# Filled slots only through an indirect gather and scatter, and the experts' down product in high and low parts, in a two-layer block with 32 experts

## The reference, cut to what matters

```python
expert_id = (grp_idx * EXPERTS_PER_GROUP + top_i).reshape(-1)      # 1024 assignments in all
weights = grp_p * top_p / jnp.sum(top_p, axis=-1, keepdims=True)
...
def expert_block(args):
    xe, e = args                                                   # the tokens of expert e
    hid = jax.nn.silu(xe @ w_gate[e]) * (xe @ w_up[e])
    return hid @ w_down[e]
...
y = jnp.einsum('tkd,tk->td', y_assign.reshape(n_tok, TOP_K, d), weights.astype(yb.dtype))
```

## Time and profile before

| | |
|---|---|
| median of 3 runs | 3261.04 us (3250.35 to 3279.0) |
| the profiled execution | 3276.96 us, its span 3275.2 us |
| PE busy | 2789.9 us (85%) |
| PE weight load busy | 1775.8 us (54%) |
| DVE busy | 1397.0 us (43%) |
| ACT busy | 1001.0 us (31%) |
| POOL busy | 177.4 us (5%) |
| HBM traffic over the span | 129 GB/s mean |

### The profile page before, as it was taken

How to read it: one execution, slowest core, us unless ns; L and a number is a source line. 1 busy time by engine, 2 the same in 40 slices (tenths; PEclk the granted TensorE clock), 3 DMA queues, 4 the chain that set the end, 5 groups by cost and what they waited for, 6 DMA issues and landing times. The chain is left out here.

```text
span 3275.2 us, 30824 instructions
## 1 busy us (share of the span) xinstructions
PE 2789.9 (85%) x10792; PEld 1775.8 (54%) x10792; DVE 1397.0 (43%) x2100; ACT 1001.0 (31%) x1619; POOL 177.4 (5%) x200
## 2 busy tenths in 40 slices
PE   7899977479999779799996999848988999698885
PEld 1455455247777547457774444424755767444442
DVE  1104177532223235532355555532563234555554
ACT  1101221132222243532222444413353222244441
POOL 0000000000000010000000212100100000021110
PEclk9899988789999889989997999978999999799997
DMA  8401110013212212012223999941111222299994
GB/s 303 137 26 52 52 49 1 30 52 103 81 47 90 81 52 78 26 67 75 78 73 112 346 319 335 317 158 52 55 49 52 90 77 67 93 328 328 323 323 143
DMA packets 262816, 419.14 MB, mean 128 GB/s; under 512 B 17503, under 2 KB 179311, under 8 KB 262639
## 3 DMA queue, kind: packets, MB, share of 16 engines
q1 hardware_dynamic: 236448, 340.55, 31.6%
q10 hardware_dynamic: 17807, 47.76, 3.9%
q0 software_dynamic: 8448, 29.37, 3.0%
HBM read 390.37 MB, written 31.20 MB: 129 GB/s over the span
## 5 line engine op out<-in xcount | busy, mean ns | idle before, releaser
L180 PE MATMUL banks<-arena_parts,hT_parts 128*128 128x512 f32 x1056 | 442.6, 419 | 37.8 <-DVE ring_parts L210 26.3
L2537 DVE TENSOR_TENSOR ring_parts<-ring,hT_parts 128x2048 fp32r<-128x2048 f32 x128 | 292.5, 2286 | 302.4 <-ACT hT_parts L2453 302.2
L182 PE MATMUL banks<-arena_parts,ring_parts 128*128 128x512 f32 x1056 | 419.5, 397 | 0.0
L156 PE MATMUL banks<-ring,arena 128*80 128x512 f32 (+3 forms) x776 | 361.0, 611 | 15.5 <-DMA ring<-in_w_mod 11.4
L180 PE MATMUL banks<-hT_parts,arena_parts 128*80 128x512 f32 (+1 forms) x816 | 336.2, 412 | 43.9 <-DVE hT_parts L2534 18.6
L210 DVE TENSOR_TENSOR ring_parts<-ring,hT_parts 128x1024 fp32r<-128x1024 f32 x148 | 181.3, 1225 | 422.2 <-ACT hT_parts L206 419.5
L181 PE MATMUL banks<-ring_parts,arena_parts 128*80 128x512 f32 (+1 forms) x880 | 355.5, 404 | 0.0
L2453 ACT ACTIVATE hT_parts<-ring 128x2048 fp32r<-128x2048 f32 x128 | 243.9, 1907 | 355.2 <-DMA ring<-in_w_exp_up 330.9
L181 PE MATMUL banks<-hT_parts 128*128 128x512 f32 x864 | 345.2, 400 | 0.0
L206 ACT ACTIVATE hT_parts<-ring 128x1024 fp32r<-128x1024 f32 x148 | 156.6, 1058 | 479.3 <-PE banks L182 478.5
L180 PEld LDWEIGHTS banks<-arena_parts,hT_parts 128*128 128x128 f32 x1056 | 200.8, 190 | 113.4 <-issue 65.5
(11 more groups left out here) (435 smaller groups left out, 3198.0 us busy)
## 6 DMA issues: line engine op xcount, KB each, us to landing
ring<-in_w_exp_gate SPq DMA_DIRECT2D x64, 1024.0 KB, 6.8
ring<-in_w_exp_up SPq DMA_DIRECT2D x64, 1024.0 KB, 10.5
ring<-in_w_exp_down SPq DMA_DIRECT2D x128, 512.0 KB, 8.5
ring<-in_w_in SPq DMA_DIRECT2D x58, 1024.0 KB, 7.1
ring<-in_w_mod SPq DMA_DIRECT2D x24, 1024.0 KB, 7.9
y_rows<-arena ACTq DMA_DIRECT2D x64, 320.0 KB, 6.1
ring<-in_w_gate SPq DMA_DIRECT2D x11, 1024.0 KB, 5.5
ring<-in_w_up SPq DMA_DIRECT2D x11, 1024.0 KB, 8.0
```

The source lines that it names most:

```text
L156: last = nc.tensor.matmul(out, l, r, start=(i == 0), stop=(i == len(pairs) - 1))
L180: nc.tensor.matmul(out, lh, rh, start=start and i == 0, stop=False)
L182: last = nc.tensor.matmul(out, ll, rh, start=False, stop=stop and i == len(terms) - 1)
L2537: return V.tensor_tensor(half_of(ring_r, n, h), half_of(ring, n, h), ew_hi[:, h, :, :].bitcast(F32), ALU.subtract)
```

## The change

**Slots.** The tables now hold the token of an assignment plus one (assignments 0 to 1023), so that an empty slot gives -1. `tok_tab` holds the token, `row_tab` the assignment, and both gather and scatter pass a bounds check that leaves an index of -1 out. The first slot of a block is always filled, with token 0 and a spare row 1024 where no token is there. The ranks of a block are spread over its partitions (`slot_rank`). Results go by an indirect scatter on POOL to `y_rows` in the order of the assignments, so the combine reads `y_rows` with eight plain DMAs on ACT. `xg` is zeroed once in each layer. The fill of spare rows of `y_rows` before the scan (`fill_act`, four DMAs, 1792 KB) is gone, and two small DMAs of POOL at the start open the semaphores `yb_out0/1`. In the routing eight small DVE operations in five dependent groups follow the table's product where one cast did, and two that made `row_i` are gone.

**Down product.** It goes through `mm3`: twelve fp32r matmuls in place of four fp32 ones. ACT makes the high part of the down weights (`down_hi`), DVE the low part in place (`down_lo`) and the low part of the turned hidden rows (`hidden_lo`).

**Row copy.** `copy_rows` moves from DVE to ACT, and waits there for the scatter of two experts before (`yb_out`).

```diff
-            def rows_out(c, w):
+            def rows_out(c, n):
+                w = dn_rows(ring_r, n)
                 for h in range(2):
-                    last = mm(ps[0:CAP, 4 + h, :], [(e_ht[:, c, f, :], w[:, f, h * HB:(h + 1) * HB]) for f in range(2)])
+                    at = slice(h * HB, (h + 1) * HB)
+                    last = mm3(ps[0:CAP, 4 + h, :], [(ht_hi[:, c, f, :], ht_lo[:, c, f, :], dn_hi[:, f, at], w[:, f, at]) for f in range(2)], True, True)
...
-            def down(b, c, n, it):
-                j, r = ex_down(n), R + it
-                landed(pe, j, r)
+            def down(b, c, n):
+                pe.wait_ge(S("ex_dl"), b + 1)
                 pe.wait_ge(S("ex_ht"), b + 1)
                 pe.wait_ge(S("ex_yb"), b + 1)
...
             def body(b, c, n, it):                      # ACT
+                d_hi(b - 1, n - 1, it)
                 w_hi(b + 1, n + 1, it, 0)
                 silu(b, c)
                 x_hi(b + 1, 1 - c)
                 w_hi(b + 1, n + 1, it, 1)
+                rows(b - 1, 1 - c)
                 copy_h(b, c)
-                store(b - 1, 1 - c)
...
             def last():                                 # ACT
                 b = NE - 1
+                d_hi(b - 1, b - 1, 0)
                 silu(b, 1)
+                rows(b - 1, 0)
+                d_hi(b, b, 0)
                 copy_h(b, 1)
-                store(b - 1, 0)
-                store(b, 1)
+                rows(b, 1)
...
             def body(b, c, n, it):                      # DVE
+                d_lo(b - 1, n - 1)
                 w_lo(b + 1, n + 1, 0)
                 mult(b, c)
                 x_lo(b + 1, 1 - c)
                 w_lo(b + 1, n + 1, 1)
-                rows(b - 1, 1 - c, n - 1, it)
+                h_lo(b, c)
...
+            def rows(b, c):                             # ACT
+                act.wait_ge(S("ex_dn"), b + 1)
+                act.wait_ge(S(f"yb_out{c}"), yb_done(b, c, lay))
+                copy_rows(c).then_inc(S("ex_yb"), 1)
...
+            def put(b, c):                              # POOL
+                g.tensor_copy(row_cur[c], column(row_tab, b))
+                pool.drain()
+                return g.indirect_dma_start(out=y_rows, out_offset=bass.IndirectOffsetOnAxis(ap=row_cur[c].bitcast(U32), axis=0),
+                                            in_=yb[:, c, :], in_offset=None, bounds_check=2 * LAT, oob_is_err=False)
...
-            with pool.Fori(0, NE // 2 - 1, 1) as it:
+            gather(2, 0)
+            gather(3, 1)
+            with pool.Fori(0, NE // 2 - 2, 1) as it:
                 for c in range(2):
-                    gather(it * 2 + (c + 2), c)
+                    gather(it * 2 + (c + 4), c)
+                    scatter(it * 2 + c, c)
+            for b in range(NE - 4, NE):
+                scatter(b, b % 2)
...
-                    g.indirect_dma_start(out=comb[:, i, j, :], out_offset=None, in_=y_rows,
-                                         in_offset=bass.IndirectOffsetOnAxis(ap=row_i[:, j * LT + i:j * LT + i + 1].bitcast(U32), axis=0)).then_inc(S(f"comb_in{i}"), 16)
+                    act.dma_start(comb[:, i, j, :], y_rows[j * LAT + i * P:j * LAT + (i + 1) * P, :]).then_inc(S(f"comb_in{i}"), 16)
```

More of the change, by code:

```diff
@@ L1321, in rope_pool, with yb_open_pool @@
             pool.drain().then_inc(S("freq_full"), 1)
[L1323 to L1327, removed]
+        def yb_open_pool(pool):
+            for c in range(2):
+                nc.gpsimd.dma_start(y_rows[2 * LAT:2 * LAT + 1, 0:P], ident[0:1, :]).then_inc(S(f"yb_out{c}"), 16)
+                pool.wait_ge(S(f"yb_out{c}"), 16)
         def rope_act(act):
@@ L2405, in body @@
                 turn_x(1 - c, n + 1, it)
-                down(b - 1, 1 - c, n - 1, it)
+                down(b - 1, 1 - c, n - 1)
                 turn_h(b, c)
@@ L2524, in experts_act, with experts_dve @@
                     act.wait_ge(S("ov_th"), k + 1)
-                    hidden_turned(0).then_inc(S("ov_ht"), 1)
-                    act.wait_ge(S("ov_yb"), k + 2)
-                    put(bass.ds(k * CAP + NE * CAP, CAP), 0).then_inc(S("ov_out"), 16)
-        def experts_dve(dve):
+                    hidden_turned(0).then_inc(S("ov_hh"), 1)
+                    act.wait_ge(S("ov_dn"), k + 2)
+                    act.wait_ge(S("ov_free"), k + 1)
+                    copy_rows(0).then_inc(S("ov_yb"), 1)
+                act.wait_ge(S("ov_free"), OVER + 1)
+            for c in range(2):
+                act.wait_ge(S(f"yb_out{c}"), yb_done(NE + c, c, lay))
+            for i in range(LT):
+                for j in range(2):
+                    act.dma_start(comb[:, i, j, :], y_rows[j * LAT + i * P:j * LAT + (i + 1) * P, :]).then_inc(S(f"comb_in{i}"), 16)
+        def experts_dve(dve, lay):
             V = nc.vector
@@ L2555, in mult, with d_lo, h_lo @@
                 hidden(c).then_inc(S("ex_hid"), 1)
-            def rows(b, c, n, it):
-                dve.wait_ge(S("ex_dn"), b + 1)
-                if n >= 2 or not isinstance(it, int):
-                    dve.wait_ge(S(f"yb_out{c}"), 16 * ((n + 2) // 2) + 16 * it)
-                copy_rows(c).then_inc(S("ex_yb"), 1)
+            def d_lo(b, n):
+                dve.wait_ge(S("ex_dh"), b + 1)
+                down_lo(ex_down(n)).then_inc(S("ex_dl"), 1)
+            def h_lo(b, c):
+                dve.wait_ge(S("ex_hh"), b + 1)
+                hidden_lo(c).then_inc(S("ex_ht"), 1)
             def first():
-                dve.sem_inc(S("ex_yb"), 1)
-                for c in range(2):
-                    dve.sem_inc(S(f"yb_out{c}"), 16)
                 x_lo(0, 0)
@@ L2636, in experts_pool @@
                     pool.sem_inc(S("ov_x"), 1)
[L2637 to L2645 removed]
+                    pool.wait_ge(S("ov_yb"), k + 2)
+                    put(k + NE, 0).then_inc(S("ov_out"), 16)
+                    pool.wait_ge(S("ov_out"), before + 16 * k + 16)
+                    pool.sem_inc(S("ov_free"), 1)
         def combine_dve(dve):
@@ L2820, in _ @@
             rope_pool(pool)
+            yb_open_pool(pool)
             rendezvous(pool, "pool")
```

134 lines of the change are left out of this document (83 added, 51 removed).

## The result

The changed kernel takes 3302.84 us (median of 4 runs, 3291.5 to 3305.84), the kernel before beside it 3258.18. The ratio is 1.0135, with a 95% interval of 1.0109 to 1.0162: slower by 1.35%, where I had forecast 1.5% faster. Its profiled execution has a span of 3303.7 us.

The account below looks back on a forecast made before the run. The DMA queue, through the landing of the gate/up weights, was taken to bound each step. 58 steps x 1.0 us = -58, edges +10, gave -48: median 3213 us, -1.5%, 8-in-10 range 3170 to 3272.

Parts of the forecast that it names:

- the cost of POOL: In each expert step, index copy, gap and issue take 3.6 us a pair, two pairs 7.1 of 10.6 us.
- second rival: POOL becomes the bound as its pairs meet VectorE's subtractions: above 5.3 us a pair, step 12.3 us, 3312 us; 8%.
- The bytes: In the expert stages, leaving out empty slots cuts DMA traffic from 3.80 to 3.41 MB a step, 10.4 us.
- first rival: Left-out rows cost the DMA engines about the same, or the loop keeps its length: step stays 11.6 us, 3271; 15%.
- The loop: Two-step loop of gate/up load, high and low parts and PE's matmuls: a step falls from 11.6 to 10.6 us.
- PE: In the expert step, twelve fp32r matmuls cut its own step from 10.62 to 9.8 us, the floor of any step.
- ScalarE: Down weights' high part and row copy raise its work from 4.9 to 7.8 us a step, costed at nothing.
- VectorE: Added subtractions, less the row copy, raise its work from 6.7 to 8.1 us a step, costed at nothing.
- third rival: Down weights land too late for ScalarE in the expert loop: +1.0 to +2.1 us a step, 3271 to 3335 us; 10%.
- The edges: Start and end of each expert layer: +5 us together (+2 to +9), two layers +10.
- the end of the loop: Row copy and high and low parts between the last two down products: +4.7 us, less 0.8 for each product.
- The combine: After the expert loop, scatter in place of store adds 2.5 us; eight gathers turned plain loads save 2 us.

Follow-up runs that it names:

- nolo: Changed kernel with VectorE's low part of the down weights left out, PE reading the high part in its place; 3292.7 us, ratio 1.0108.
- table: Changed kernel without POOL's index copies and drains, indirect DMAs reading the table's columns, POOL's loop written out; 3217.74 us, ratio 0.9861.
- sem: Changed kernel with each drain between index copy and indirect DMA replaced by the copy's own semaphore, POOL's loop written out; 3209.0 us, ratio 0.9843.
- onedrain: Changed kernel with both index copies of a step ahead of one shared drain, POOL's loop written out; 3204.12 us, ratio 0.9832.
- down: Kernel before with only the down product in parts and the row copy on ScalarE; slots, gather and store as before; 3290.49 us, ratio 1.0085.
- downbusy: Same as down, with one extra unused fp32 matmul behind each down product to keep PE busy; 3282.39 us, ratio 1.007.
- best: Changed kernel with one drain a step for both index copies and the last expert's down product in plain fp32 matmuls; 3195.3 us, ratio 0.981.

## Why the prediction was wrong

**The step that failed** is the cost of POOL: "With 0.2 for the copy and 1.0 for the gap that is 3.6 us, twice 7.1 of 10.6." I took the gap between copy and DMA as a constant, from one row, where it is the time that the previous indirect DMA still has to land, with 0.9 us on top. In the changed kernel, in the mean of all 64, the gather pair takes 0.98 (copy) + 4.2 (gap) + 1.2 (issue) = 6.3 us and the scatter pair 0.39 + 3.6 + 1.6 = 5.5, together 11.9 against steps of 12.1 and 12.3. The lesson is in the same sentence: I added durations of an engine where a latency had to be asked for. My second rival had the place and the decision point right (POOL bound above 5.3 us a pair, here 5.9; row copies that wait for `yb_out`, here 75.8 us in 24 steps; time forecast 3312, measured 3303), and the mechanism wrong: `nolo` shows that VectorE's lock isn't it. That its time came out near is luck.

**The bytes** were right: 3.39 MB a step where I had 3.41, and q0 carried 16.81 MB in 64 steps, 0.263 a step where I had 0.26. The first rival, rows left out that cost as much, fell: q0 held 1.6% of 3303.7 us for 16.81 MB, 3.1 us a MB, where it held 10.4% of 310 us for 8.85 MB before, 3.6 us a MB; and without the drain the DMA share is 0.97 to 1.00 at 10.4 to 10.6 us a step.

**The loop** was right as soon as POOL was free. (The first window of the earlier trace rows ends 1.5 us behind the start of the thirtieth row copy; to that start it is 334.67 us and not 336.15, 11.5 us a step and not 11.6, which hardly moves the sum.) I had 10.6 us a step; `table`, `sem` and `onedrain` have 10.6, 10.5 and 10.4. ScalarE's wait for the gate/up landing was to fall from 5.5 to 2 to 3 us a step, and is 61.5 us in 25 waits, 2.5, in `sem`. My 3213 us lies between `table` and `sem`: the forecast fits the kernel that the change would be without the two drains.

**PE** in `sem` is busy 281.69 us in 29 steps, 9.7, forecast 9.8. **ScalarE** is busy 7.6 us of a step and **VectorE** 8.0 there, 8.2 in the changed kernel (forecast 7.8 and 8.1); the row copy takes 1.02 us, and I had put it at 1.0 between 0.69 and 1.91. The third rival, down weights that land too late, isn't what cost time: in the windows of the changed kernel, `table` and `sem` the high part of the down weights never waited, and in `down` and `downbusy` never for a landing.

**The clock** is a term that my sum didn't have. Where the down product in parts frees PE and nothing uses the time, the clock goes from 0.98 and 0.99 to 0.94 and 0.93, and in the traces half of what `down` loses in its windows comes back with it. In the changed kernel it falls to 0.94 and 0.92 as PE waits for rows; with POOL free it is 0.99 and 1.00. It follows the stall; the 24 gate/up matmuls take 6.1 us there as in `sem`, and no run shows that the lower clock cost time there.

**The edges**, by the starts of rows (us, first and second layer):

| from, to | before | changed | `best` |
|---|---|---|---|
| first gather, first row copy | 34.4, 33.5 | 31.7, 30.7 | 32.1, 30.0 |
| 29 steps | 334.7, 336.9 | 350.3, 357.3 | 303.0, 300.6 |
| row copy 30 to 31 | 8.3, 7.9 | 9.6, 8.5 | 9.8, 9.9 |
| row copy 31 to 32 | 5.0, 5.0 | 10.7, 10.1 | 5.0, 5.0 |
| last row copy, first matmul of the combine | 15.5, 12.7 | 13.3, 9.4 | 14.8, 10.1 |
| sum | 397.9, 396.1 | 415.7, 416.0 | 364.7, 355.5 |

At the end of the loop I had +4.7 less 1.6, and it is +5.4 on average with another +1 an interval earlier: the parts stood on the path nearly whole. The combine I had at +2.5 - 2, and it is -2.2 and -3.3, plain loads for gathers being worth more than the scatter costs. A gain of 2.7 and 2.9 at the start of a stage I hadn't seen. In sum the edges of the changed kernel came to +2.1 and -0.5 us a layer from the first gather on, where I had +3.6 of my +5 there: a small miss that alters nothing.

Of the 37.7 us that the two stages lost between the profiled executions, 36.0 are in the windows. The medians differ by 44.7 us and the spans by 28.5, as the profiled execution of the kernel before lay 19 us above its median and that of the changed kernel 3 us above its own; much of this difference lies ahead of the first expert stage (its first gather stands at 1764.84, that of the changed kernel at 1754.46).

## What to carry to other kernels

When a change puts a second DMA of a kind on an engine's queue, ask what each instruction between them waits for, and look in the trace for the place where two already follow each other closely; a gap that varies (0.84 here, 3.54 there) is a wait and not a cost. Between an index copy and its indirect DMA, wait for the copy's own semaphore, or put one drain ahead of both DMAs of a step. And TensorE made faster without being the bound can lose its clock, as in `down`, so look at the granted clock before calling such a part free.

## What the runs showed of the hardware

- POOL's drain behind an indirect DMA lasts until that DMA has landed: its record ends 0.07 to 0.08 us after the landing and the next indirect DMA starts 0.85 to 0.90 us after it, in 118 cases of 118 (0.90 to 0.91 with two copies ahead of the drain); with a semaphore on the copy the gap is 0.78 to 0.82 us in 125 cases of 128, 0.91 at most.
- Rows left out by the bounds check cost next to nothing on the DMA engines: q0 carries 16.81 MB at 1.6% of the span, 3.1 us a MB against 3.6 without rows left out, and windows of 3.4 MB a step run at 319 to 330 GB/s.
- TensorE's granted clock fell from 0.98 and 0.99 to 0.94 and 0.93 in the two stages of `down`, where each step had about 0.8 us less work for it (an estimate: 3.6 us of fp32 matmuls less twelve at 0.234), and one further matmul a step brought it back to 0.99 and 0.98.
